# Output projection and last down projection in two passes of two thirds and one third, with the layers written out

## The reference, cut to what matters

```python
def trunk_layer(l, x, c, samp, W):
    mod = silu(c) @ w_ada[l] + b_ada[l]
    sh1, sc1, g1, sh2, sc2, g2 = split(mod, 6)
    h = rmsnorm(x, g_norm1[l]) * (1 + sc1) + sh1
    p = h @ w_in[l] + b_in[l]
    ...                       # three head groups: mLSTM, pooling, forgetting attention
    x = x + g1 * (concat(ha, hb, hc) @ w_out[l])
    h2 = rmsnorm(x, g_norm2[l]) * (1 + sc2) + sh2
    x = x + g2 * (square(relu(h2 @ w_up[l])) @ w_down[l])
```

## Time and profile before

| what | us |
|---|---|
| median of the runs | 3036.97 (3034.89 to 3041.54) |
| the profiled execution | 3036.13 |
| its span in the profile | 3034.4 |
| TensorE busy | 2813.1 (93%) |
| VectorE / ScalarE / GpSimd busy | 1205.3 / 681.6 / 463.8 |
| mean granted TensorE clock | 0.960 |

### The profile page before, as it was taken

One profiled execution on the slowest core, in us unless ns is written; L12 is line 12 of the kernel. 1 busy time (PEld: TensorE's weight loads), 2 busy tenths in 40 slices (PEclk: granted clock), 3 DMA queues, 4 the chain that ended last, 5 costly groups with the idle time before them and its releaser, 6 DMA issues. The chain is left out here.

```text
span 3034.4 us, 49785 instructions
## 1 busy us (share of the span) xinstructions
PE 2813.1 (93%) x20776; PEld 2586.1 (85%) x20776; DVE 1205.3 (40%) x2114; ACT 681.6 (22%) x1165; POOL 463.8 (15%) x472
## 2 busy tenths in 40 slices
PE   4899978889999999999969999788899999999997
PEld 2899965569999999999969998455899999999996
DVE  2625523355632423324335353233564233242333
ACT  2434323333211111000133442233231111100011
POOL 0110104341100000000011000334320000000000
PEclk9999978889999999999979999788999999999998
DMA  7431147741122221111134102875312222211111
GB/s 280 152 86 32 59 174 257 254 139 51 49 85 90 88 87 63 49 42 49 42 119 128 36 29 80 285 236 189 106 37 90 84 84 84 84 49 42 49 43 77
DMA packets 103307, 308.15 MB, mean 102 GB/s; under 512 B 19845, under 2 KB 27910, under 8 KB 100626
## 3 DMA queue, kind: packets, MB, share of 16 engines
q1 hardware_dynamic: 102914, 304.09, 30.0%
q0 software_dynamic: 160, 0.79, 0.1%
HBM read 282.21 MB, written 22.63 MB: 100 GB/s over the span
## 5 line engine op out<-in xcount | busy, mean ns | idle before, releaser
L446 PE MATMUL PS<-aH,whi 128*128 128x352 f32 x1632 | 534.8, 328 | 18.2 <-DVE aL L392 18.2
L446 PE MATMUL PS<-hH,whi 128*128 128x352 f32 x1632 | 537.3, 329 | 14.5 <-DVE wlo L439 8.5
L446 PE MATMUL PS<-hL,whi 128*128 128x352 f32 x1632 | 525.6, 322 | 0.0
L446 PE MATMUL PS<-hH,wlo 128*128 128x352 f32 x1632 | 525.1, 322 | 0.0
L446 PE MATMUL PS<-aL,whi 128*128 128x352 f32 x1632 | 525.0, 322 | 0.0
L446 PE MATMUL PS<-aH,wlo 128*128 128x352 f32 x1632 | 524.5, 321 | 0.0
L434 POOL CAST whi<-raw 128x1024 fp32r<-128x1024 f32 x174 | 185.7, 1068 | 1772.6 <-PE PS L446 1344.0
L446 PEld LDWEIGHTS PS<-aH,whi 128*128 128x128 f32 x1632 | 307.9, 189 | 26.6 <-issue 26.6
L446 PEld LDWEIGHTS PS<-hH,whi 128*128 128x128 f32 x1632 | 308.5, 189 | 23.9 <-DVE wlo L439 8.7
L446 PEld LDWEIGHTS PS<-hL,whi 128*128 128x128 f32 x1632 | 309.0, 189 | 0.5 <-issue 0.5
L446 PEld LDWEIGHTS PS<-aL,whi 128*128 128x128 f32 x1632 | 308.4, 189 | 0.0
(11 more groups left out here) (316 smaller groups left out, 3549.7 us busy)
## 6 DMA issues: line engine op xcount, KB each, us to landing
KVp<-kv SPq DMA_DIRECT2D x256, 384.0 KB, 4.1
raw<-w_ff SPq DMA_DIRECT2D x128, 512.0 KB, 3.7
wad_single<-w_ada SPq DMA_DIRECT2D x64, 512.0 KB, 3.5
raw<-w_in SPq DMA_DIRECT2D x42, 512.0 KB, 3.5
wad<-w_ada SPq DMA_DIRECT2D x32, 512.0 KB, 5.7
wada<-w_first SPq DMA_DIRECT2D x12, 1024.0 KB, 8.7
x_spill<-x SPq DMA_DIRECT2D x2, 4224.0 KB, 15.6
x<-x_spill SPq DMA_DIRECT2D x6, 1408.0 KB, 7.3
```

The lines of the kernel that those rows point to most:

```text
L446: last = nc.tensor.matmul(PS[:, 3 * p + part, 0:CW], w[:, k, :], a[:, k, part * CW:(part + 1) * CW], start=k == 0 and w is wh and a is hig ...
```

## The change

Output panels and the last eight down panels now run in two passes: first two thirds of the tokens (704 columns, one eviction for two PSUM banks), then the last third. The norm of the first two thirds is made beside the second pass, by `phase_norm`, which sums the squares in rows, takes root and reciprocal on a quarter of the columns, spreads the reciprocals into PSUM by matmuls, and makes scale, high and low in one instruction each (scale on VectorE, high on ScalarE, low on VectorE). After the last down panels this is the norm of the next layer, whose first two weight panels are loaded and split there too; in the last layer it is the final norm, whose rows are stored as they come. `projection` of the second layer begins with the last third's sums and goes on with two thirds of its first panels (`begun`). `final` and the loop are gone: the layers are written out, addresses are constants. In the last layer conditions stop after panel 17. The cut diff:

```diff
-        def spot(n):
-            return n % 2 if n < paired else 0
-
...
-            return 16 * sum(spot(i) == spot(n) for i in range(n + 1))
+            return 16 * sum(spot(i) == spot(n) for i in range(landed_before, n + 1))
 
         def load(sp, n):
-            if n >= 2:
-                sp.wait_ge(s["split"], n - 1 if n <= paired else n)
+            before = max((m for m in range(n) if spot(m) == spot(n)), default=-1)
+            if before >= 0:
+                sp.wait_ge(s["split"], before + 1)
...
+        def sums(pe, ph):
+            w = WIDE[ph] // 4
+            for src in (S[f"sums{ph}"], S["square1"]):
+                for g in range(4):
+                    last = nc.tensor.matmul(PS[32 * g:32 * g + 32, 6, 0:w], c("ones")[:, 0:32], src[:, w * g:w * (g + 1)],
+                                            start=src is not S["square1"], stop=src is S["square1"], skip_group_check=True)
+            last.then_inc(N["summed"], 1)
+
+        def spread(pe, ph):
+            w = WIDE[ph] // 4
+            pe.wait_ge(N["inverted"], first + ph + 1)
+            for half in range(2):
+                for g in (half, 2 + half):
+                    r = slice(32 * g, 32 * g + 32)
+                    out = PS[:, 3 + g // 2, w * half:w * half + w] if ph == 0 else PS[:, 6 + g // 2, P + w * half:P + w * half + w]
+                    last = nc.tensor.matmul(out, con[r, CONST["head"]][:, 0:P], S[f"roots{ph}"][r, :], start=True, stop=True, skip_group_check=True)
+                last.then_inc(N["spread"], 1)
+                pe.wait_ge(N["spread"], 2 * (first + ph) + half + 1)
+
+        def root(act, ph):
+            act.wait_ge(N["summed"], first + ph + 1)
+            nc.scalar.activation(S[f"roots{ph}"][:], PS[:, 6, 0:WIDE[ph] // 4], ACT.Sqrt, bias=c("eps")).then_inc(N["rooted"], 1)
+
+        def invert(dve, ph):
+            dve.wait_ge(N["rooted"], first + ph + 1)
+            nc.vector.reciprocal(S[f"roots{ph}"][:], S[f"roots{ph}"][:]).then_inc(N["inverted"], 1)
+
+        def scale(dve, ph, k):
+            i = KT * (first + ph) + k
+            if k == 0:
+                dve.wait_ge(N["spread"], 2 * (first + ph) + 2)
+            free = (2, 4)[ph]
+            if k >= free:
+                dve.wait_ge(N["low"], i - free + 1)
+            nc.vector.scalar_tensor_tensor(pairs(ph, buffer(ph, k)[:]), pairs(ph, x[:, k, COLS[ph]]), mod[:, sc + k, 0:1], spread_to(ph),
+                                           ALU.mult, ALU.mult).then_inc(N["scaled"], 1)
+
+        def high(act, ph, k):
+            act.wait_ge(N["scaled"], KT * (first + ph) + k + 1)
+            nc.scalar.activation(dh[:, k, prompt(ph)], buffer(ph, k)[:, 0:tokens(ph)], ACT.Identity, bias=mod[:, sh + k, 0:1]).then_inc(N["high"], 1)
+
+        def low(dve, ph, k):
+            dve.wait_ge(N["high"], KT * (first + ph) + k + 1)
+            r = prompt(ph)
+            nc.vector.scalar_tensor_tensor(dl[:, k, r], buffer(ph, k)[:, 0:tokens(ph)], mod[:, sh + k, 0:1], dh[:, k, r].bitcast(F32),
+                                           ALU.add, ALU.subtract).then_inc(N["low"], 1)
+
...
+        def finish(dve, link):
+            for k in range(KT):
+                scale(dve, 1, k)
+                if k == 1:
+                    samples(dve, link)
+                if k >= 2:
+                    low(dve, 1, k - 2)
+            low(dve, 1, KT - 2)
+            low(dve, 1, KT - 1)
+        return sums, spread, root, invert, scale, high, low, finish
...
+                    pe.wait_ge(s["split"], 2)
+                    sums(pe, 1)
+                    for part in range(NCH):
+                        if part == NCH - 1:
+                            pe.wait_ge(N["few"], 1)
+                        for n in range(2):
+                            for k in range(KT):
+                                if part == NCH - 1 and n == 0:
+                                    pe.wait_ge(N["low"], k + 1)
+                                last = part_product(n, part, k, aH, aL)
+                                if part == 0 and n == 0 and k == 5:
+                                    spread(pe, 1)
+                            last.then_inc(s["done"], 1)
+                else:
...
+                if begun:
+                    root_part(act, 1)
+                    for k in range(KT):
+                        high_part(act, 1, k)
+                else:
+                    root(act, N)
...
+                if begun:
+                    dve.sem_inc(s["split"], 2)
+                    invert_part(dve, 1)
+                    finish_norm(dve, link)
...
-        tiles_beside = {3: (0, 1), 4: (2,), 5: (3, 4), 6: (5, 6), 7: (7,)}
+
+        tiles_beside = {2: (0,), 3: (1, 2), 4: (3,), 5: (4, 5), 6: (6,), 7: (7,)}
...
-        ada_of = lambda n: (n + 6,) if 10 <= n < CONDS - 6 else ()
+        ada_of = lambda n: (n + 6,) if 10 <= n < (18 if last_layer else CONDS - 6) else ()
...
+                for n in range(2, AHEAD):
...
+                        sp.wait_ge(ada_rows, 24 if last_layer else CONDS)
...
+                if last_layer:
+                    for ph in range(2):
+                        for k in range(KT):
+                            sp.wait_ge(N["scaled"], KT * (2 + ph) + k + 1)
+                            sp.dma_start(y[:, k, COLS[ph]], out_rows[:, k, COLS[ph]]).then_inc(stored, 16)
+                    sp.wait_ge(stored, 32 * KT)
...
-                def norm_high(part, k):
-                    i = KT * part + k
-                    pool.wait_ge(N["modded"], i + 1)
-                    nc.gpsimd.tensor_copy(hH[:, k, prompt(part)], third_plain[i % 4][:, 0:width(part)]).then_inc(N["high"], 1)
-
...
+                def by_phases(run, operands, ready):
+                    n0 = START_OF[run]
+                    sums, spread = (mid, end)[run][0:2]
+                    if run:
+                        pe.wait_ge(s["split"], n0 + 1)
+                        pe.wait_ge(s["room"], NCH * (n0 - 1))
+                        for k in range(KT):
+                            ready(0, k)
+                            for part in range(2):
+                                last = part_product(n0 % 2, part, k, *operands, home(n0))
+                        last.then_inc(s["done"], 2)
+                        wide = [(j, part) for j in range(1, KT) for part in range(2)]
+                    else:
+                        wide = [(0, 0), (1, 0), (0, 1), (1, 1)] + [(j, part) for j in range(2, KT) for part in range(2)]
+                    for j, part in wide:
+                        pe.wait_ge(s["split"], n0 + j + 1)
+                        if j >= 2:
+                            pe.wait_ge(s["room"], NCH * n0 + 2 * (j - 1))
+                        elif run:
+                            pe.wait_ge(s["room"], NCH * (n0 - 1 + j))
+                        third(n0 + j, part, operands, (lambda k: ready(part, k)) if j == 0 else None)
+                    for j in range(KT):
+                        if j == 0:
+                            ready(NCH - 1, KT - 1)
+                        if j >= 2:
+                            pe.wait_ge(s["room"], NCH * n0 + 2 * KT + j - 1)
+                        third(n0 + j, NCH - 1, operands)
+                        if j == 0:
+                            pe.wait_ge(N["added"], (KT - 2) * (2 * run + 1))
+                            pe.wait_ge(N["squared"], KT * (2 * run + 1))
+                            pe.wait_ge(s["room"], NCH * n0 + 2 * KT)
+                            sums(pe, 0)
+                        if j == 1:
+                            spread(pe, 0)
+
+                def late_sums(run):
+                    pe.wait_ge(N["added"], (KT - 2) * (2 * run + 2))
+                    pe.wait_ge(N["squared"], KT * (2 * run + 2))
+                    (mid, end)[run][0](pe, 1)
...
+                    if part == NCH - 1:
                         pe.wait_ge(N["few"], 1)
                     for n in (up(0, 0), up(0, 1)):
-                        by_tile = part == NCH - 1 and n == up(0, 0)
-                        third(n, part, (hH, hL), (lambda k: pe.wait_ge(N["low"], KT * (NCH - 1) + k + 1)) if by_tile else None,
-                              (lambda: sum_third(NCH - 1)) if part == 0 and n == up(0, 0) else None)
+                        pe.wait_ge(s["split"], n + 1)
+                        pe.wait_ge(s["room"], NCH * KT)
+                        if part == 0 and n == up(0, 1):
+                            pe.wait_ge(N["low"], KT)
+                        third(n, part, (hH, hL), (lambda k: pe.wait_ge(N["low"], (KT if part == NCH - 1 else 0) + k + 1)) if part != 1 and n == up(0, 0) else None,
+                              (lambda: late_sums(0)) if part == 0 and n == up(0, 0) else None)
+                        if part == 0 and n == up(0, 1):
+                            mid[1](pe, 1)
...
+                def empty(run, ph, j):
+                    n = START_OF[run] + j
+                    if j >= 2:
```

(77 more changed lines are left out.)

418 lines of the change are left out of this document (174 added, 244 removed).

## The result

| | us |
|---|---|
| before, median of 4 | 3038.94 (3034.89 to 3041.54) |
| after, median of 4 | 2961.84 (2960.14 to 2966.55) |
| ratio | 0.975, 95% interval 0.9732 to 0.9767 |
| profiled execution after, and its span | 2963.39, 2961.6 |

The account below looks back on a forecast made before the run. TensorE was taken as the bound, busy nearly throughout 3034.4 us. Terms -23.5 - 24.0 - 18.2 + 5.2 - 14.3 - 2.0 = -76.8 took the profiled 3036.1 us to 2959.3, range 2946 to 2982.

Parts of the forecast that it names:

- conditions: Last layer's up and down panels: dropping 24 condition tiles at 0.98 us each saves 23.5 us on TensorE's path.
- boundary (meeting and second projection): Between the layers: 31.7 us lost before shrinks to 7.7, so -24.0 us, bounds -20 to -26.
- output stages: Output panels through second up panel: 18.8 us lost shrinks to 9.7, so -9.1 a layer, -18.2 us in all.
- last down panels: Last down panels of both layers: sums and spread come onto TensorE's path, 1.1 + 1.5 a layer, +5.2 us.
- end: From the last product to the span's end: 26.7 us becomes 12.2, entered as -14.3 us (12 to 16).
- fixed addresses (attention): SyncE's cached-page issues: constant layer index saves a tenth of a microsecond on 16 pages a layer, taken as -2 us.
- the loss of 2.2 us at the start: Start of the second layer's projection: the half-clock loss of 2.2 us stays, within the boundary's 7.7.
- VectorE's 3.64 us a panel: Output stage's second pass: VectorE needs 3.64 us on most panels against 3.82 available, so it keeps up.
- little to spare: Output stage's second pass: VectorE's 3.64 us against 3.82, with the waits in between, holds, but narrowly.
- The meeting did not stay at 4.5 and the weights did not bind: Rival: boundary meeting still 4.5 us and first output pass waits for weights as before: 2969 us; chance 0.10.
- The slower case: Rival: VectorE and GpSimd hold each other up in wide passes, deciding from 6.2 us an iteration; 3045 us; chance 0.02.
- rival (a): VectorE paces second passes at 5.0 us an iteration, costing 28 us: 2987; chance 0.13 together with another rival.

Follow-up runs that it names:

- experiment 2: The kernel before with its layer loop written out and without the last layer's 24 unread condition tiles: 3006.03 us, ratio 0.989.
- experiments 1 to 3: experiment 1, experiment 2, and the changed kernel with last down panels and final norm as before, output stage kept in two passes: 2986.44 us, ratio 0.9833.
- experiment 7: The changed kernel with each wide scaling of a second pass and each wide row of the final norm made twice: 2983.81 us, ratio 0.9817.
- experiment 5: The changed kernel with the third projection panel's weight cast and panel 0's eviction, first layer, waiting for panel 0 alone: 2956.36 us, ratio 0.9721.
- experiment 4: The changed kernel with only the eviction of the first layer's projection panel 0 waiting for panel 0 alone: 2963.62 us, ratio 0.9763.
- experiment 1: The kernel before with the layer loop written out and nothing else: 3028.02 us against 3037.55, ratio 0.9972.
- experiment 8: The changed kernel with the high halves of the output stage's norm made by GpSimd instead of ScalarE: 2975.81 us, ratio 0.979.
- Experiments 5 and 6: experiment 5, and on top of it the eighth chunk's head transposes moved behind the 17th panel's third part: 2956.56 us, ratio 0.9724.

## Why the prediction was right, and where it was not

| term | forecast | measured in the stages |
|---|---|---|
| conditions | -23.5 | -23.5 |
| boundary (meeting and second projection) | -24.0 | -20.7 |
| output stages | -18.2 | -16.9 |
| last down panels | +5.2 | +4.8 |
| end | -14.3 | -14.9 |
| fixed addresses (attention) | -2.0 | -4.3 |
| first projection and start | none | +2.8 |
| sum, and the span | -76.8 | -72.8 |

The medians moved by 77.1. The profiled execution of after lies 1.6 above its median, that of before 2.8 below its own. So it is luck that the medians moved by nearly the 76.8 forecast: the working is of the profiled executions, and between these the gain was 4 us short of it, with errors of both signs in its terms. The mechanisms held in the main; what was mis-sized, missing or not shown is below.

**Conditions.** One interval of evictions times a count, exact to the tenth, and additive (experiment 2). The panels on either side showed the price in the kernel before.

**Boundary.** Counted from E, where the last third's eviction starts (1529.7), the steps to the first product came out as written: low half E+2.9 (2.65 forecast), sums E+3.8 (3.8), without the loop's jump 0.8 to 0.9 us of meeting (1.1), no wait in the spread, no wait in the third part. What was mis-sized is the clock: I let the loss of 2.2 us at the start stay and it did (0.50 from 1532.5 to 1539.3), but in the rest of the second projection two stretches of 3.4 us at half clock came in, of which before had none. In after:

```profile
1665.60:1669.00 3.40, 3.40 (x14) 3.40 (x14) 1.31 (x7) 2.76 (x5) 0.29 (x1) 0.50 0.00 0
1846.50:1849.90 3.40, 3.40 (x14) 3.40 (x13) 3.13 (x14) 0.00 (x0) 0.00 (x0) 0.50 0.01 2
```

At 0.293 us instead of 0.159 a product each costs 1.6 us, 3.1 of the 3.3 missing. They come in different places in the other kernels, the first projections of experiments 1 to 3 included, with a stop of 1.9 us right in front in some cases (116.0 in after) and none near in others (1665.6 and 1846.5 here), while other stops of 1.9 us had none behind them (366.8 in after). Where exactly they come I can not tell from these runs.

**Output stage.** 9.1 forecast, 8.3 to 8.6 measured. The waits for weights that I had left at 1.5 are nothing, and the 0.5 before sums too. Against that stand two waits of 0.7, for the mix's low half and before the first up panel, and a longer half-clock start: products come 0.29 us apart until 668.8, 8.0 us from the first one at 660.8, and before it was 4.7 (658.4 to 663.1); 3.3 us more at that pace lose 1.5. The 0.3 for bank changes is a term that no row shows. VectorE's 3.64 us a panel was 3.80 with no idle time, since its wide instructions came 0.86 us apart and not 0.80, and it lags 2.0; one of the signs I gave, that it would wait for ScalarE's evictions, came in panels 1 and 2 alone (2.2 and 2.5 us). It held for the reason given, and experiment 7 shows how far: 7.5 us more in a pass are not felt in it, but behind it, as a stop of 6.0 us and a restart at half clock. That is the better account of the margin than "little to spare": the pass has a buffer of two panels, the norm behind it none.

**Down panels and end.** 2.4 a layer for the sums and spread (2.6 forecast). At the end the working itself, 26.7 less 12.2, gives 14.5 and not the 14.3 that went into the sum; measured 14.9. E+8.7 forecast for the last row was E+9.6 (2949.7 to 2959.3), and the tail from there 2.3 us instead of 3.3, with stores of a third of the size.

**Fixed addresses.** Per issue the term was put too high (0.05, not 0.1), and yet attention is shorter by more than the 2.0: 4.3 in after, and over all eighteen stages behind the change of the loop 242.2 us in the mean against 244.5. Twenty-two issues give 1.1 us of that a layer; the rest goes in part with the granted clock (the shortest stages have 0.85, before 0.82) and in part with the waits for pages, and whether either is owed to the change is open. The term's sign came true; that it came by the quicker issues is not shown.

**What was missed.** One term was not in the working at all: the wait `5` in `freed` and `emptied_first`, written for the second layer's order of parts, also acts in the first, where the parts are reported all at once. It delays a cast by panel 1's last nine products: 1.4 us of stop and a stretch at half clock, 2.6 us together (experiment 5). My first reading of it, from the releaser, was wrong (experiment 4).

**The rivals.** VectorE did not pace the passes (experiment 7). The meeting did not stay at 4.5 and the weights did not bind (experiment 1, the waits above). The slower case asked for an iteration of 6.2 us; even with GpSimd beside every panel, as experiment 8 had it, VectorE's panels were 5.2 us apart at most from panel 3 on (6.6 in the one before, which has a weight subtraction) and the kernel stayed well under before. That is about the pace rival (a) had asked for, and it cost the output stages 9.3 and 8.7 us, where (a) had 7 a pass. Of the change as made, the high halves on ScalarE are a part without which the output stage in two passes would give nothing: 208.7 us against 208.2.

Experiments 5 and 6 are the fastest versions, 2956.36 and 2956.56; experiment 5 has two changed waits for it.

## What to carry to other kernels

Count the idle and foreign time of the bound engine stage by stage, give each its price from an interval next to it, and the sum of a large rewrite can come out within a few us (here 4 of 77, with errors of both signs). A pass that makes the next stage's input beside itself can lag by as much as its buffers allow, and everything it lags is paid at its end, so look at what the last tile waits for. When a wait count is changed for a new order of parts, go through every path that still uses the old order, and do not trust the engine named in a wait on several semaphores until an edit has moved it.

## What the runs showed of the hardware

- A loop's jump back cost 3.6 us at a meeting of all engines (4.5 against 0.8 to 0.9).
- The granted clock fell to 0.50 for single stretches of 3.4 us amid dense products, behind stops of 1.9 us or with no stop near; each cost 1.6 us. Attention stages with the same work took 239.6 to 246.8 us, at a granted clock of 0.82 to 0.85 that explains only a part of the difference.
- GpSimd's `tensor_scalar` with 704 fp32 columns took 2.07 us where ScalarE's activation took 0.88. A VectorE instruction with two SBUF inputs took 1.06 us instead of 0.55 when it started 0.15 us behind GpSimd's, and its usual 0.55 when it started 1.0 us behind it; one with an input in PSUM was not slowed.
